# Making a small Gelu from the exponential inside an attention loop, and moving what follows by two steps

## The chip, the cores and the metric

The kernel runs on one core of a Trainium2 chip. The metric is the device time of one execution in microseconds, the median of several runs. Below, PE is TensorE, ACT is ScalarE, DVE is VectorE and POOL is GpSimd.

## The reference, cut to what matters

Two transformer blocks run one after the other on 512 tokens of width 1024, in float32. The second one holds a sparse attention with three branches. The change touches the smallest of them, the compressed branch, in which keys and values of 32 tokens are squeezed into one by a small two-layer network:

```python
def compress_blocks(kr, pos, w1, b1, w2):
    nc = (T - CMP_BLOCK) // CMP_STRIDE + 1            # 31 windows
    idx = np.arange(nc)[:, None] * CMP_STRIDE + np.arange(CMP_BLOCK)[None, :]
    blk = kr[:, idx] + pos[None, None, :, None, :]
    flat = blk.transpose(0, 1, 3, 2, 4).reshape(B, nc, G, CMP_BLOCK * D)
    return jax.nn.gelu(flat @ w1 + b1) @ w2           # hidden width 256; gelu is the tanh form
```

It is called once for keys and once for values. The hidden layer is 256 wide, for two groups of 31 windows each: as the kernel holds it, 128 partitions by 2 (keys, values) x 2 (halves of 256) x 62 = 248 numbers.

## The kernel before, in words

Each large matmul takes its float32 operands as a high and a low part, so that a product is three matmuls: a weight unit of 128x1024 comes by DMA into one of six slots of `stage`, ACT rounds it to `w_hi` (L657), POOL forms `w_lo` as two instructions of 128x512 (L683), and PE uses both.

The second attention (`at2`) is written out by hand as a loop over steps. It has 96 items (a head, a block of 128 queries and a key range). PE, ACT, DVE and POOL each run their own loop over the same step numbers, and wait for each other through semaphores. In step n:

- PE issues the logits of items n and n+1 when n is even (L1074), then the value products of the pair n-6 (`soft_heads`, L1096), the transposes of items n-4 and n-3 (L1121), then a number of matmuls from a list of other work (`FILL2`), and last its hooks. The fill matmuls are the query and key projections of the same layer (`pe_chunk_steps`, L1424): each projection is 24 matmuls into one PSUM bank (bank 6), and the next one waits until DVE has read the bank (`dve_evac2`, L1035).
- DVE runs its early hooks (`dve0`; each `dve_evac2` is one), scales and adds the bias to item n (L1276), normalises item n-1 after ACT's exponential (L1298, L1304), and then runs its late hooks (`dve`).
- ACT takes the exponential of item n-1 (L1211), copies the transposed weights of item n-4 for PE (L1229), and runs its hooks.
- POOL only runs its hooks.

The compressed branch lives in these hooks. `at` is 49, the step in which its first layer's last matmuls are transposed (`pe_hidden`). The Gelu stands at ACT's step 50 (`act_gelu`, L1687), the second layer at PE's step 52 (`pe_second`, L1696 and L1701), its copies at ACT's step 53 (`act_second`), its logits on PE at 54 and 57 (`pe_cmp_s`, L1731), their scaling on DVE at 55 and 58 (`dve_cmp_logits`, L1754), the softmax's steps on DVE from 59 to 66 (`dve_cmp_shift` at 59 and 61, L1764 to L1768; `dve_cmp_probs` at 63 and 65, L1784 to L1792; `dve_cmp_weigh`), its transposes on PE at 66 and 68, the value products on PE at 70, 72, 74 and 76 (`pe_cmp_pv`, L1828), the sums on DVE one step after each (`dve_cmp_add`, L1837), and the split of the result into high and low parts at 78 to 82 (`act_sum_hi`, `dve_sum_lo`). The fill's projections `kb`, `qb0`, `qb1`, `qb2` and `qb3` are read by DVE at the start of steps 52, 56, 64, 72 and 85; the output projection begins as fill in step 86.

Of the kernel before, what the change touches and what calls it, by code (L numbers as in the profile page):

```python
# [35 lines left out]
ALU = mybir.AluOpType  # L36
ACT = mybir.ActivationFunctionType
# [24 lines left out]
NCMP = (T - CMP_BLOCK) // CMP_STRIDE + 1  # L62
# [97 lines left out]


IN_BLOCKS = 68
FILL2 = [0, 8] * 24 + [0, 12] * 4 + [0, 6] * 6 + [3] * 4 + [0] + [2] * 12 + [0]
FILL2 = FILL2 + [4, 3] * 5 + [2, 4, 3, 4, 3, 3]


def fill2_steps(name):

    return sum(12 if n in CMP_AT else 24 for n in FILL2_TASKS[:FILL2_TASKS.index(name) + 1])


def filled(table, count):

    total = 0
    for n, f in enumerate(table):
        total += sum(f) if isinstance(f, tuple) else f
        if total >= count:
            return n
    raise AssertionError(count)
# [6 lines left out]
def turn_steps(g):  # L186

    return 4 * (g + 1) + 3 * max(0, g - 1)
# [22 lines left out]
def build(nc, weights, x_t, params, rows, table_t, bias_line, out_t):  # L211
    with ExitStack() as top:
        def sem(name):
            return top.enter_context(nc.semaphore(name))

        def sb(name, shape, dtype=F32, ctx=top):
            return ctx.enter_context(nc.sbuf_tensor(name, shape, dtype))
# [54 lines left out]
        with ExitStack() as scope:  # L272
# [5 lines left out]
            scratch = sb("scratch", [P, 2 * T], ctx=scope)  # L278
# [21 lines left out]
            hid = sb("hid", [P, 2, 2, 2 * NCMP], ctx=scope)  # L300
# [48 lines left out]
        PS = top.enter_context(nc.psum_tensor("PS", [P, 8, T], F32))  # L349

        def pc(name, k, n=1):
            a, _ = PARAMS[name]
            return par[:, a + k:a + k + n]
# [305 lines left out]
        def act_next(act, u):  # L659

            act_hi(act, u + AHEAD)
# [235 lines left out]
        def queries2(p):  # L897
            return HOME2[f"q{p}" if p < 4 else f"qb{p - 4}"]
# [24 lines left out]
        for p, (kind, c) in enumerate(GROUPS1):  # L923
            q, k = chunk1(2 * p), chunk1(2 * p + 1)
            groups1.append(len(items1))
            for i in reversed(range(TB)) if p == 7 else range(TB):
# [7 lines left out]
                else:  # L934
                    for m in range(2):
                        h = 2 * c + m
# [6 lines left out]
        for p in range(8):  # L943
            c, q = p % 4, queries2(p)
            groups2.append(len(items2))
            for i in range(TB):
                if p < 4:
                    k0, nk, s0 = full(i)
                    for branch in range(2):
                        k = HOME2[("ks", "kw")[branch]]  # L950
                        for g in range(2):
                            h = 4 * g + c
# [6 lines left out]
                else:  # L959
                    k0, nk = max(i - 1, 0) * P, min(i + 1, 2) * P  # L960
                    k = HOME2["kb"]
                    for g in range(2):
                        h = 4 * g + c
# [6 lines left out]
        for items in (items1, items2):  # L970
            pre, at = 0, 0
# [12 lines left out]
        class Attn:  # L984
# [14 lines left out]
        at2 = Attn("at2", items2, groups2, SCALE)  # L999
        qk_evac = [sem("qk_evac1"), sem("qk_evac2")]  # L1000
        ITEM_PS = 3
        cm = {k: sem("cm_" + k) for k in (
            "raw", "kp", "kp_hi", "kp_lo", "mlp", "pre_t", "hid", "kv", "kv_sb", "none", "blank", "z", "zz", "s", "l", "e", "p", "t", "pt", "pv", "used")}
# [10 lines left out]
        def hook(a, engine, step, what):  # L1014
            a.hooks[engine].setdefault(step, []).append(what)
# [9 lines left out]
        for ci in range(4, 16):  # L1025
            at = filled(FILL1, 24 * (ci - 3)) + 1
            hook(at1, "dve0", at, lambda dve, ci=ci: dve_chunk(dve, ci))
            at = NEXT_LATE.get(ci, at + 1)
# [8 lines left out]
        for e, name in enumerate(FILL2_TASKS):  # L1037
            at = filled(FILL2, fill2_steps(name)) + 1
            hook(at2, "act", at + 1, lambda act, u=U_FILL2 + e: act_next(act, u))
# [15 lines left out]
        def pe_attn(pe, a, fill=None, per_item=()):  # L1055
# [6 lines left out]
            def logits(n):  # L1062

                it = items[n]

                pair = [it] if it.kind == "diff" else [it, items[n + 1]]
                maps = [(x, m) for x in pair for m in range(len(x.maps))]
                if it.map0 >= 2:
                    pe.wait_ge(a.s_read, it.map0 - 1)
                for cols in pieces(it.nk):  # L1070
                    last = cols.stop == it.nk
                    for x, m in maps:
                        q, k = x.maps[m]
                        mm = pe.matmul(PS[:, x.bank[m], cols], q, k[:, cols], start=True,  # L1074
                                       stop=(not last or x.kind != "sb"))
                        if last and (x.kind == "soft" or m == 1):
                            mm.then_inc(a.qk_done, 1)
                if it.kind == "sb":
                    for x, m in maps:
                        pe.matmul(PS[:, x.bank[0], x.nk - P:x.nk], ident_r[:, :], mask_r[:, :],  # L1080
                                  start=False, stop=True).then_inc(a.qk_done, 1)
# [42 lines left out]
            if a is at2:  # L1124
                for n in range(len(items) + 6):
# [5 lines left out]
                    if n < len(items) and n % 2 == 0:  # L1131
                        logits(n)
                    if n < IN_BLOCKS:
                        if n >= 6 and n % 2 == 0:
# [455 lines left out]
        for g in range(SPARED):  # L1590
            at = filled(FILL1, 24 * 12 + turn_steps(g)) + 1
            hook(at1, "pool", at, lambda pool, g=g: pool_turn1(pool, g))
        for p in range(8):
            at = groups1[p + 1] if p < 7 else len(items1)
            hook(at1, "pool", at + 4, pool_head_square(p))
            hook(at1, "pool", at + 7, pool_head_scale(p))
        for p in range(7):
            at = groups1[p + 1] + 4
# [6 lines left out]
        for g in range(6):  # L1605
            at = filled(FILL1, 24 * 12 + turn_steps(g)) + 1
# [34 lines left out]
        def pool_windows(s):  # L1641

            def what(pool):
                pool.wait_ge(cm["raw"], 64 * (s + 1))
                if s == 1:
                    wait_unit(pool, fill2_unit("cmp_k3"))
                win = bass.AP(tensor=kpair.tensor, offset=kpair.offset,
                              ap=[kpair.ap[0], [2, 16], [T, 2], [CMP_STRIDE, NCMP]])
                pos = pc("pos_k" if s == 0 else "pos_v", 0, 16).unsqueeze(2).unsqueeze(3).to_broadcast([P, 16, 2, NCMP])
                pool.tensor_tensor(kp.rearrange("p j (g c) -> p j g c", g=2), win, pos, ALU.add).then_inc(cm["kp"], 1)  # L1650
            return what
# [13 lines left out]
        def act_hidden(s):  # L1665
            def what(act):
                act.wait_ge(cm["raw"], 64)
                wait_unit(act, fill2_unit(("cmp_k3", "cmp_v3")[s]))
                act.activation(hidden(s), PS[0:2 * NCMP, 7, 0:CMP_HID], ACT.Copy).then_inc(cm["mlp"], 1)
            return what  # L1670
# [11 lines left out]
        def act_gelu(act):  # L1682
            act.wait_ge(cm["pre_t"], 1)
            for s in range(2):
                for half in range(2):
                    at = s * CMP_HID + half * P
                    act.activation(hid[:, s, half, :], PS[:, 7, at:at + 2 * NCMP], ACT.Gelu_apprx_tanh,  # L1687
                                   bias=pc("b1_k" if s == 0 else "b1_v", half)).then_inc(cm["hid"], 1)
            act.preload_act_table_set("natural_log_exp_and_others")

        def pe_second(pe):

            pe.wait_ge(cm["hid"], 4)
            for g in range(2):
                for half in range(2):
                    pe.matmul(PS[g * HD:(g + 1) * HD, 7, P:P + NCMP], pc("w2_k", half * HD, HD),  # L1696
                              hid[:, 0, half, g * NCMP:(g + 1) * NCMP], start=(half == 0), stop=(half == 1))
            for i in range(4):
                for g in range(2):
                    for half in range(2):  # L1700
                        mm = pe.matmul(PS[32 * i:32 * i + NCMP, 7, g * HD:(g + 1) * HD],  # L1701
                                       hid[:, 1, half, g * NCMP:(g + 1) * NCMP], pc("w2_v", half * HD, HD),
                                       start=(half == 0), stop=(half == 1))
            mm.then_inc(cm["kv"], 1)
# [143 lines left out]
        hook(at2, "dve0", groups2[4], lambda dve: dve.wait_ge(swa_done, 4))  # L1848
        hook(at2, "dve", filled(FILL2, fill2_steps("q3")) + 4, dve_swa_late)
        for s, at in ((0, filled(FILL2, fill2_steps("kc")) + 5), (1, filled(FILL2, fill2_steps("cmp_k3")))):  # L1850
            hook(at2, "pool", at, pool_windows(s))
            hook(at2, "act", at + 3, act_windows(s))
            hook(at2, "pool", at + 4, pool_windows_lo(s))
        for s in range(2):
            hook(at2, "act0", filled(FILL2, fill2_steps(("cmp_k3", "cmp_v3")[s])) + 1, act_hidden(s))
        at = filled(FILL2, fill2_steps("cmp_v3")) + 2
        hook(at2, "pe", at, pe_hidden)
        hook(at2, "act", at + 1, act_gelu)
        hook(at2, "dve0", at + 2, dve_blank_values)
        hook(at2, "pe", at + 3, pe_second)  # L1860
        hook(at2, "act", at + 4, act_second)
        for half in range(2):
# [851 lines left out]
```

## Time and profile before

| | |
|---|---|
| median of 3 runs | 1612.85 us (1612.77 to 1612.92) |
| the profiled execution | 1612.32 us, of which the profile's span is 1610.5 us |
| PE busy | 1589.0 us, 99% of the span |
| PE weight loads | 84% |
| DVE, POOL, ACT busy | 60%, 55%, 47% |
| the second attention's steps 48 to 96 | about 1111 to 1215 us of the span |

PE is busy nearly throughout, so what counts is when PE stands idle and who ends that. The clock granted to PE is full in every slice of the page.

### The profile page before, as it was taken

The page shows a single profiled execution, that of the slowest core. Times are in us where ns is not written, and L with a number is a line of the kernel's source. Part 1 is how long each engine was busy: PE and PEld are TensorE (multiplying, and loading weights), DVE is VectorE, ACT ScalarE, POOL GpSimd, SP SyncE. Part 2 cuts the span into 40 slices and gives each one's busy share as a digit, 9 for nine tenths or more (in the row PEclk, how much of TensorE's full clock was granted, in tenths as well). Part 3 has the DMA queues.
Part 4 walks back from the last instruction along what each step waited for, and adds up shares of the span by engine and source line. Part 5 has one row for each costly group of instructions (what it writes and reads, how often), then busy time and mean ns, then how long its engine had stood idle before and what let it go on. Part 6 is the DMA issues. An engine that isn't in the chain of part 4 may idle for free.

```text
span 1610.5 us, 23966 instructions
## 1 busy us (share of the span) xinstructions
PE 1589.0 (99%) x9196; PEld 1351.1 (84%) x9196; DVE 966.2 (60%) x1592; ACT 761.2 (47%) x1391; POOL 886.7 (55%) x641
## 2 busy tenths in 40 slices
PE   9999999999999999999999999999999999999997
PEld 8787878888888888889998887877767889999886
DVE  7176756884444225878884434576783587886224
ACT  6366655543344324545554323577573445555222
POOL 7424354575445553558889553654114548889650
PEclk9999999999999999999999999999999999999999
DMA  5411103322323222323333222322012323233221
GB/s 209 151 53 53 40 14 105 117 93 93 104 92 104 93 95 76 105 93 105 105 106 105 93 95 74 120 93 80 27 28 92 99 98 105 96 103 106 96 100 53
DMA packets 49682, 147.56 MB, mean 92 GB/s; under 512 B 5152, under 2 KB 13728, under 8 KB 49568
## 3 DMA queue, kind: packets, MB, share of 16 engines
q1 hardware_dynamic: 48232, 143.39, 26.8%
q10 hardware_dynamic: 1336, 2.63, 0.5%
q8 instruction: 74, 1.21, 0.3%
q14 instruction: 40, 0.33, 0.1%
HBM read 142.84 MB, written 3.41 MB: 91 GB/s over the span
## 4 chain that ended last, share of the span: by engine, by line
PE 81%; DVE 2%; POOL 1%; ACT 1%; issue 1%; DMA 1%; SPq 0%; DVEq 0%; ACTq 0%
PE PS L621 14%; PE PS L623 14%; PE PS L622 14%; PE PS L2154 7%; PE PS L2155 6%; PE PS L2156 6%; PE PS L1413 4%; PE PS L582 4%; PE PS L1424 3%; PE PS L590 2%; PE PS L1074 2%; PE PS L1096 2%; PE PS L1121 1%; POOL w_lo L683 1%; DMA stage<-in_weights 1%
## 5 line engine op out<-in xcount | busy, mean ns | idle before, releaser
L683 POOL TENSOR_TENSOR w_lo<-stage,w_hi 128x512 fp32r<-128x512 f32 x402 | 567.3, 1438 | 598.6 <-ACT w_hi L657 597.7
L657 ACT ACTIVATE w_hi<-stage 128x1024 fp32r<-128x1024 f32 x262 | 270.5, 1054 | 303.3 <-DMA stage<-in_weights 289.4
L621 PE MATMUL PS<-H_hi,w_hi 128*128 128x512 f32 x512 | 199.4, 389 | 0.4 <-DVE rcol L1622 0.4
L622 PE MATMUL PS<-H_lo,w_hi 128*128 128x512 f32 x512 | 199.3, 389 | 0.0
L623 PE MATMUL PS<-H_hi,w_lo 128*128 128x512 f32 x512 | 199.2, 389 | 0.0
L621 PE MATMUL PS<-A_hi,w_hi 128*128 128x512 f32 x496 | 193.2, 389 | 0.6 <-DVE A_lo L829 0.6
L623 PE MATMUL PS<-A_hi,w_lo 128*128 128x512 f32 x496 | 193.0, 389 | 0.0
L622 PE MATMUL PS<-A_lo,w_hi 128*128 128x512 f32 x496 | 193.0, 389 | 0.0
L2128 POOL TENSOR_TENSOR S_lo<-S_f,S_hi 128x512 fp32r<-128x512 f32 x90 | 126.5, 1421 | 66.5 <-DVE S_f L1988 37.7
L2128 POOL TENSOR_TENSOR w_lo<-stage,w_hi 128x512 fp32r<-128x512 f32 x90 | 141.8, 1603 | 0.0
L2154 PE MATMUL PS<-F,w_hi 128*128 128x256 f32 x480 | 137.5, 287 | 1.7 <-ACT conv L2047 1.1
L829 DVE TENSOR_TENSOR A_lo<-A_all,A_hi 128x512 fp32r<-128x512 f32 x40 | 52.7, 1321 | 139.6 <-ACT A_hi L765 139.6
L2155 PE MATMUL PS<-F,w_hi 128*128 128x256 f32 x480 | 135.8, 283 | 0.0
L621 PEld LDWEIGHTS PS<-H_hi,w_hi 128*128 128x128 f32 x512 | 96.1, 188 | 20.5 <-DVE rcol L1622 0.7
L623 PEld LDWEIGHTS PS<-H_hi,w_lo 128*128 128x128 f32 x512 | 96.1, 188 | 20.1
L622 PEld LDWEIGHTS PS<-H_lo,w_hi 128*128 128x128 f32 x512 | 96.1, 188 | 20.0
L621 PEld LDWEIGHTS PS<-A_hi,w_hi 128*128 128x128 f32 x496 | 93.1, 188 | 20.8 <-DVE A_lo L829 1.5
L622 PEld LDWEIGHTS PS<-A_lo,w_hi 128*128 128x128 f32 x496 | 93.1, 188 | 19.3
L623 PEld LDWEIGHTS PS<-A_hi,w_lo 128*128 128x128 f32 x496 | 93.1, 188 | 19.2
L2154 PE MATMUL PS<-F,S_hi 128*128 128x256 f32 x360 | 101.9, 283 | 0.0
L2155 PE MATMUL PS<-F,S_hi 128*128 128x256 f32 x360 | 101.9, 283 | 0.0
L2156 PE MATMUL PS<-F,S_lo 128*128 128x256 f32 x360 | 101.9, 283 | 0.0
(295 smaller groups left out, 3583.2 us busy)
## 6 DMA issues: line engine op xcount, KB each, us to landing
stage<-in_weights SPq DMA_DIRECT2D x254, 512.0 KB, 3.4
stage<-in_weights SPq DMA_DIRECT2D x32, 128.0 KB, 2.8
out_t<-Y SPq DMA_DIRECT2D x8, 256.0 KB, 2.0
X<-in_x_t SPq DMA_DIRECT2D x3, 512.0 KB, 8.4
bias_line<-bias_line ACTq DMA_DIRECT2D x1, 1270.0 KB
strip<-bias_line ACTq DMA_DIRECT2D x1, 1024.0 KB, 5.0
stage<-in_weights SPq DMA_DIRECT2D x2, 256.0 KB, 4.1
V<-QF SPq DMA_DIRECT2D x4, 128.0 KB, 2.7
```

Source lines behind the costliest of these rows:

```text
L582: pe.matmul(PS[:, j, :], w[:, (u0 + j) % RING, bass.ts(c, P)], H_hi[:, c, :], start=(k == 0 and w is w_hi), stop=False)
L621: pe.matmul(out, a, h_hi, start=first, stop=False, skip_group_check=skip)
L622: pe.matmul(out, a, h_lo, start=False, stop=False, skip_group_check=skip)
L623: return pe.matmul(out, b, h_hi, start=False, stop=last, skip_group_check=skip)
L657: act.activation(w_hi[:, slot, :], stage[:, slot, :], ACT.Copy).then_inc(hi_done, 1)
L683: lo = pool.tensor_tensor(w_lo[:, slot, cols], stage[:, slot, cols], w_hi[:, slot, cols].bitcast(F32), ALU.subtract)
L829: dve.tensor_tensor(halves_lo(inst, f), product(inst, f), halves_hi(inst, f).bitcast(F32), ALU.subtract).then_inc(a_lo_done, 1)
L1413: mm = pe.matmul(PS[:, j, :], w[:, u % RING, cols], h, start=(g == 0 and x == 0), stop=(g == 7 and x == 2))
L2128: return pool.tensor_tensor(out, raw, hi.bitcast(F32), ALU.subtract)
L2154: pe.matmul(bank, hi[:, cols], where[:, h, k, :], start=(first and k == 0), stop=False, skip_group_check=True)
L2155: pe.matmul(bank, hi[:, cols], where[:, l, k, :], start=False, stop=False, skip_group_check=True)
L2156: mm = pe.matmul(bank, lo[:, cols], where[:, h, k, :], start=False, stop=(k == 3), skip_group_check=True)
```

## The change

The four Gelu instructions become four Identity instructions that only add the bias and bring the hidden layer from PSUM to SBUF. From there x * gelu's factor is worked out as x / (1 + exp(-2 c (x + 0.044715 x^3))): four instructions on POOL form the exponent's argument and bound it, ACT takes the exponential one step later, and three on DVE add one, take the reciprocal and multiply. The request for the exponential's table behind the Gelu goes. All hooks of the branch from `pe_second` on stand two steps later; the projections and the rest of the loop stay where they were.

```diff
+GELU_STEPS = 2
...
-                    act.activation(hid[:, s, half, :], PS[:, 7, at:at + 2 * NCMP], ACT.Gelu_apprx_tanh,
+                    act.activation(hid[:, s, half, :], PS[:, 7, at:at + 2 * NCMP], ACT.Identity,
                                    bias=pc("b1_k" if s == 0 else "b1_v", half)).then_inc(cm["hid"], 1)
-            act.preload_act_table_set("natural_log_exp_and_others")
...
+        def gelu_parts():
+
+            x = hid[:, :, :, :].rearrange("p s h c -> p (s h c)")
+            return x, scratch[:, 0:8 * NCMP]
+
+        def pool_gelu(pool):
+
+            x, t = gelu_parts()
+            pool.wait_ge(cm["hid"], 4)
+            pool.tensor_tensor(t, x, x, ALU.mult).then_inc(cm["hid"], 1)
+            pool.wait_ge(cm["hid"], 5)
+            pool.tensor_scalar(t, t, 2.0 * GELU_C * 0.044715, 2.0 * GELU_C, ALU.mult, ALU.add).then_inc(cm["hid"], 1)
+            pool.wait_ge(cm["hid"], 6)
+            pool.tensor_tensor(t, t, x, ALU.mult).then_inc(cm["hid"], 1)
+            pool.wait_ge(cm["hid"], 7)
+            pool.tensor_scalar(t, t, EXP_BOUND, None, ALU.max).then_inc(cm["hid"], 1)
+
+        def act_gelu_exp(act):
+
+            _, t = gelu_parts()
+            act.wait_ge(cm["hid"], 8)
+            act.activation(t, t, ACT.Exp, scale=-1.0).then_inc(cm["hid"], 1)
+
+        def dve_gelu(dve):
+
+            x, t = gelu_parts()
+            dve.wait_ge(cm["hid"], 9)
+            dve.tensor_scalar(t, t, 1.0, None, ALU.add).then_inc(cm["hid"], 1)
+            dve.wait_ge(cm["hid"], 10)
+            dve.reciprocal(t, t).then_inc(cm["hid"], 1)
+            dve.wait_ge(cm["hid"], 11)
+            dve.tensor_tensor(x, x, t, ALU.mult).then_inc(cm["hid"], 1)
...
-            pe.wait_ge(cm["hid"], 4)
+            pe.wait_ge(cm["hid"], 12)
...
         hook(at2, "act", at + 1, act_gelu)
+        hook(at2, "pool", at + 1, pool_gelu)
+        hook(at2, "act", at + 2, act_gelu_exp)
+        hook(at2, "dve", at + 2, dve_gelu)
         hook(at2, "dve0", at + 2, dve_blank_values)
+        at += GELU_STEPS
         hook(at2, "pe", at + 3, pe_second)
```

On DVE, at the end of step 51 and the start of step 52, these rows stood in a row before (`small`, `stat` are columns of statistics, `B_f` is the home of projection `kb`, `QF` holds the compressed values):

```order
L1710 MEMSET QF 128x512
L1276 ISA L,stat<-PS,strip 128x128
L1276 ISA stat 128x1
L1298 RECIPROCAL stat<-stat 128x1
L1304 TENSOR_SCALAR tmp<-tmp,stat,gates 128x128
L1035 TENSOR_TENSOR B_f<-PS,rstd 128x512
L1276 ISA L,stat<-PS,strip 128x256
```

and these now (lines behind the new functions have other numbers):

```order
L1746 MEMSET QF 128x512
L1277 ISA L,stat<-PS,strip 128x128
L1277 ISA stat 128x1
L1299 RECIPROCAL stat<-stat 128x1
L1305 TENSOR_SCALAR tmp<-tmp,stat,gates 128x128
L1721 TENSOR_SCALAR scratch<-scratch 128x248
L1723 RECIPROCAL scratch<-scratch 128x248
L1725 TENSOR_TENSOR hid<-hid,scratch 128x248
L1036 TENSOR_TENSOR B_f<-PS,rstd 128x512
```

The three new instructions stand ahead of the read of `kb`'s bank.

On ACT, from the end of step 50 to step 52, these stood before:

```order
L1229 ACTIVATE O<-PS 128x512
L1687 ACT_TABLE_LOAD
L1687 ACTIVATE hid<-PS,par 128x62 x4
L1689 ACT_TABLE_LOAD
L1211 ACTIVATE tmp,stat<-L,stat 128x128
L1229 ACTIVATE O<-PS 128x512
L1211 ACTIVATE tmp,stat<-L,stat 128x128
```

and these now:

```order
L1230 ACTIVATE O<-PS 128x512
L1688 ACTIVATE hid<-PS,par 128x62 x4
L1212 ACTIVATE tmp,stat<-L,stat 128x128
L1230 ACTIVATE O<-PS 128x512
L1715 ACTIVATE scratch<-scratch 128x248
L1212 ACTIVATE tmp,stat<-L,stat 128x128
```

Both table loads are gone, and the new exponential stands behind step 51's copy for PE.

On PE, at the end of step 52 and the start of step 53, these stood before:

```order
L1121 MATMUL PS<-ident,sq 128x128 x2
L1696 MATMUL PS<-hid,par 64x31 x4
L1701 MATMUL PS<-par,hid 31x64 x16
L1424 MATMUL PS<-H_hi,w_hi 128x512
L1424 MATMUL PS<-H_lo,w_hi 128x512
```

and these now:

```order
L1122 MATMUL PS<-ident,sq 128x128 x2
L1425 MATMUL PS<-H_hi,w_hi 128x512
L1425 MATMUL PS<-H_lo,w_hi 128x512
L1425 MATMUL PS<-H_hi,w_lo 128x512
```

The second layer has left the place ahead of projection `qb0`'s first matmul; it now follows the transposes of step 54.

## Rows read from the trace of the kernel before

**Rows 1.** Who PE waited for, 1080 to 1290 us: us in total, times, longest

```profile
PE PS L1096 <- ACT O L1229: 1.4, 1, 1.4
PE PS L1424 <- DVE QB L1035: 0.6, 1, 0.6
```

**Rows 2.** Timeline of PE, steps 52 and 53 (start, duration in us)

```profile
1121.82 1.09 PE L1096 MATMUL PS<-O,V 128*64 128x128 f32 x16 [1.38 <-ACT O L1229]
...
1123.22 0.43 PE L1696 MATMUL PS<-hid,par 128*64 128x31 f32 x8
...
1124.90 0.50 PE L1424 MATMUL PS<-H_hi,w_hi 128*128 128x512 f32 x1
```

**Rows 3.** Timeline of ACT, steps 50 and 51

```profile
1117.26 1.28 ACT L1687 ACT_TABLE_LOAD   x1
1118.56 0.92 ACT L1687 ACTIVATE hid<-PS,par 128x62 f32<-128x62 f32 x4
1119.50 1.28 ACT L1689 ACT_TABLE_LOAD   x1
...
1121.19 0.58 ACT L1229 ACTIVATE O<-PS 128x512 f32<-128x512 f32 x1
```

**Rows 4.** Timeline of DVE, steps 50 to 52

```profile
1115.45 1.05 DVE L1304 TENSOR_SCALAR sq<-sq,stat,gates 128x128 f32<-128x128 f32 x1
...
1121.32 0.17 DVE L1298 RECIPROCAL stat<-stat 128x1 f32<-128x1 f32 x1 [4.05 <-ACT tmp L1211]
...
1121.78 0.68 DVE L1035 TENSOR_TENSOR B_f<-PS,rstd 128x512 f32<-128x512 f32 x1
```

**Rows 5.** Timeline of POOL, 1105 to 1140 us

```profile
1113.91 2.51 POOL L683 TENSOR_TENSOR w_lo<-stage,w_hi 128x512 fp32r<-128x512 f32 x2 [0.43 <-ACT w_hi L657]
1125.17 2.54 POOL L683 TENSOR_TENSOR w_lo<-stage,w_hi 128x512 fp32r<-128x512 f32 x2 [8.75 <-ACT w_hi L657]
```

**Rows 6.** Groups by line and shape, whole span (busy us, mean ns)

```profile
L1539 POOL TENSOR_TENSOR scratch<-O 128x512 f32<-128x512 f32 x8 | 8.5, 1064 | 0.5 <-POOL O L1561 0.5
L1359 POOL CAST H_hi<-turn_f 128x512 fp32r<-128x512 f32 x4 | 2.4, 612 | 5.9 <-ACT turn_f L1351 5.7 <-POOL O L1553 0.2
L2307 POOL CAST cdist<-hid 128x128 f32<-128x128 int32 x1 | 0.8, 760 | 0.0
L1196 ACT ACTIVATE L<-L 128x256 f32<-128x256 f32 x8 | 3.3, 418 | 0.3
L1844 DVE TENSOR_SCALAR V<-V 128x256 f32<-128x256 f32 x4 | 0.9, 280 | 0.0
L1632 DVE RECIPROCAL gates<-gates 128x96 f32<-128x96 f32 x1 | 0.8, 752 | 0.0
L1788 DVE RECIPROCAL small<-small 128x16 f32<-128x16 f32 x2 | 0.5, 254 | 0.1
```

**Rows 7.** Timeline of DVE, steps 58 to 64

```profile
1140.73 0.86 DVE L1754 SCALAR_TENSOR_TENSOR L<-cdist,PS 128x124 f32<-128x124 f32 x4
...
1142.57 0.66 DVE L1764 TENSOR_REDUCE small<-L 128x16 f32<-128x496 f32 x1
...
1144.07 0.68 DVE L1276 CUSTOM_DVE_ANT_0 L<-PS,strip 128x512 f32<-128x512 f32 x1
...
1151.09 0.66 DVE L1784 TENSOR_REDUCE small<-L 128x16 f32<-128x496 f32 x1
...
1152.39 0.68 DVE L1035 TENSOR_TENSOR QB<-PS,rstd 128x512 f32<-128x512 f32 x1
```

**Rows 8.** Timeline of PE, steps 60 and 76

```profile
1142.13 1.13 PE L1074 MATMUL PS<-K_f,QF 64*128 64x256 f32 x8
...
1176.17 1.09 PE L1828 MATMUL PS<-scratch,QF 128*64 128x128 f32 x16
```

**Rows 9.** Timeline of DVE, steps 78 and 85

```profile
1179.31 0.48 DVE L1276 CUSTOM_DVE_ANT_0 L<-PS,V,row 128x256 f32<-128x256 f32 x1 [0.62 <-PE PS L1074]
...
1190.25 0.68 DVE L1035 TENSOR_TENSOR QB<-PS,rstd 128x512 f32<-128x512 f32 x1
```

More of the change, by code:

```diff
@@ L1686, in act_gelu @@
                     at = s * CMP_HID + half * P
-                    act.activation(hid[:, s, half, :], PS[:, 7, at:at + 2 * NCMP], ACT.Gelu_apprx_tanh,
+                    act.activation(hid[:, s, half, :], PS[:, 7, at:at + 2 * NCMP], ACT.Identity,
                                    bias=pc("b1_k" if s == 0 else "b1_v", half)).then_inc(cm["hid"], 1)
-            act.preload_act_table_set("natural_log_exp_and_others")
+        EXP_BOUND = -80.0
+        GELU_C = math.sqrt(2.0 / math.pi)
+        def gelu_parts():
[23 more added lines that the diff above has]
+            dve.tensor_tensor(x, x, t, ALU.mult).then_inc(cm["hid"], 1)
         def pe_second(pe):
-            pe.wait_ge(cm["hid"], 4)
+            pe.wait_ge(cm["hid"], 12)
             for g in range(2):
```

## The prediction

> **What bounds the kernel now.** I read the busy shares first: PE is busy 99% of the span, so only what makes PE stand idle, or what adds matmuls, can move the time, and the change adds no matmul. Then I read who PE waits for between 1080 and 1290 us, the second attention and the start of what follows. The longest wait of PE there is one of 1.4 us for ACT's copy, and the next is one of 0.6 us for DVE's read of a projection bank [rows 1]. Then the timelines around both. The first stands right behind the two table loads: ACT loads the Gelu's table at 1117.26, runs four instructions in 0.92 us, loads the old table until 1120.78, takes step 51's exponential, and only then makes the copy, 1121.19 to 1121.77 [rows 3], for which PE waited 1.38 us; PE had been ready at 1121.82 - 1.38 = 1120.44 [rows 2]. So the loads are on the path that sets the end, but PE's own work hides all of them except 1.38 us. After the last output projection the next weights are requested when PE frees their slots, so a shift of PE in this attention moves the rest of the span with it.
>
> **The change part by part.**
> *Removed: two table loads.* ACT's four instructions now start at 1117.26 and end at 1118.18, and the copy of step 51 follows as before 1121.19 - 1120.78 = 0.41 us after them, ready at about 1119.2 (before 1120.44) [rows 2, 3]. The wait of 1.38 us goes; the gain from it is at most that. PE then reaches the end of step 52's transposes at 1123.22 - 1.38 = 1121.84 [rows 2].
>
> *Moved: the second layer.* It took PE from 1123.22 to 1124.90, 1.68 us [rows 2], between these transposes and the first matmul of `qb0`. It now comes in step 54: it costs the same there, but it no longer covers DVE. PE wants the bank of `kb` at 1121.84, not at 1124.90. Before, DVE had read it at 1122.46 (1121.78 + 0.68) [rows 4], 2.4 us early.
>
> *Added: the chain POOL, ACT, DVE.* It starts at 1118.18. POOL is free: its last work ended at 1116.42, and its next came at 1125.17 [rows 5]. POOL's two products are like L1539, a square of 128x512 in 1064 ns: by columns 248/512 x 1064 = 0.52, with a fixed part for each I take 0.56 us. For a tensor-scalar instruction on POOL there is no row; nearest with one input is the cast, 612 ns for 512 columns [rows 6]. By columns alone that is 0.30, with L1539's price it is 0.56; I take 0.40, nearer to the cast. Sum 2 x 0.56 + 2 x 0.40 = 1.92, and 0.06 to 0.08 for each of four hand-overs (POOL starts 0.08 us behind ACT in the timelines): the argument is ready at about 1120.4. The ends are 1.6 us (all by columns) and 2.8 us (all four at the rate of L683 at its slower mean of 1.44 us, 0.70 each). ACT's exponential is L1196's size: 0.42, to 1120.9 [rows 6]. ACT stands still for it from about 1119.2; behind it wait the exponential of item 51 and the copy of item 48, which PE's transposes release only near 1121.9, so nothing is late there.
>
> DVE: the add is 0.28 (L1844). The reciprocal is what counts: 254 ns for 16 columns and 752 ns for 96, so 498/80 = 6.2 ns a column, and for 248 columns 752 + 152 x 6.2 = 1.70 us [rows 6]; its low end is 0.75, the row of 96 columns itself. The product of 248 columns I put at 0.41, from the read of 512 columns of B_f at 0.68 [rows 4], of which half the columns is 0.34 at least. With hand-overs DVE runs from 1120.96 to 1123.4. Behind these three stands the read of `kb` (0.68): done at 1124.03, and PE goes on at 1124.08.
>
> So at equal work: PE begins `qb0` at 1124.08 instead of 1124.90, but still owes the 1.68 us of the second layer: 1124.08 + 1.68 - 1124.90 = **+0.86 us**. PE's wait for ACT of 1.38 us is replaced by one of 2.24 us for DVE (1124.08 - 1121.84). Ends: with the short reciprocal and POOL's low end -0.4, with POOL's high end +1.7.
>
> *A rule weighed.* While POOL's pair of instructions ran until 1116.42, a DVE instruction that began at 1115.45 took 1.05 us and ended in the same moment, 1116.5 [rows 4, 5]; it is 0.3 to 0.4 us long when POOL rests. In the changed kernel the normalisation of item 50 on DVE falls at about 1119, among POOL's four. If DVE has to wait, it is free again long before 1120.96, so I price it at nothing; if instead POOL waits for DVE, the chain grows by one such instruction, 0.35 us. The Trainium skill says in SBUF — State Buffer, section "SBUF: two separate sides", that the shared port pair is an exclusive lock for which whichever instruction started first makes the other stand still; by that rule the sum would be 0.35 us more at worst, and the trace agrees for the side that it shows.
>
> *Two steps later, first stretch.* Up to step 64 DVE is the late one: PE waited 0.6 us for its read of `qb1` [rows 1]. From item 60 (1144.07) to that read (1152.39) DVE needed 8.32 us. Of this `dve_cmp_probs` (1151.09 to 1152.39, 1.30) now comes after it; `dve_cmp_logits` (0.86 less an overlap of 0.08) and one `dve_cmp_shift` (1142.57 to 1144.07, 1.50), which lay before item 60, come into it [rows 7]: 8.32 - 1.30 + 0.78 + 1.50 = 9.30. But DVE can start item 60 at 1143.2, when its logits end [rows 8], and not at 1144.07: 1152.5 against 1152.39, so **+0.1 us**.
>
> *Second stretch.* In steps 78 to 85 DVE works without rest and PE waits for it. One value product of PE (1176.17, 1.02 net of overlap [rows 8]) moves from step 76 to 78, behind the logits of item 78, for which DVE had waited until 1179.31 [rows 9]: DVE starts that stretch 1.0 us sooner. It has one sum more in it (`dve_cmp_add`, 0.6). So its read of `qb3` at 1190.25 [rows 9] comes 0.4 us sooner, and with it the output projection: **-0.4 us**. If DVE is not free by 1178.3, this turns into up to +0.6. The splits at 79 to 82 move to 81 to 84, all still ahead of that read, and cost nothing more.
>
> *Sum:* 0.86 + 0.1 - 0.4 = +0.5 us. The profiled execution (1612.32) would be at 1612.8; the median stands 0.53 above it, so 1612.85 + 0.5 = **1613.3 us**.
>
> **The rivals.**
> *The wait is simply gone* (15%). If DVE's three instructions are short (a reciprocal of 0.75) and POOL's at their low end, PE's wait for `kb` is near 2.24 - 0.95 - 0.3 = 1.0 us, and with the second stretch the kernel gains about 0.8: 1612.0. If DVE would read the bank ahead of the chain, the whole 1.38 would be kept: 1611.1. Against it: the two reciprocal rows lie on one line that leaves little room, and the order on DVE is fixed.
> *The later stretches pay* (20%). DVE is busy nearly without gaps from 1140 on, and small instructions on it grow when POOL forms a low part. If the two-step shift puts more on DVE just before `qb2`'s read and before step 78, PE waits 0.4 there, the -0.4 is lost and the +0.6 comes: 1613.3 + 0.4 + 0.4 + 0.6 = 1614.7.
> *POOL is far slower* (6%), the side of slower by over 0.2%. One row of POOL, a cast of 128 columns, took 760 ns [rows 6], 5.9 ns a column; at that rate the four instructions take 5.9 us, not 1.92, the chain ends 4 us later, and all of it is PE's wait: 1617.3. It decides from where the four take 1.92 + 2.7 = 4.6 us. Against it: that cast converts integers, and every float row is at 1.2 to 2.8 ns a column.
> The Trainium skill, GPSIMD Engine Reference, section 3.1, gives about 2.6 cycles an element for a product of two tensors on this engine, an estimate of 0.54 us for 248 columns, which the rows bear out.
>
> **How the numbers follow.** The forecast (a DVE wait of about 2.2 us in place of ACT's, net 0 to +1.4) has 55%, the rivals 15, 20 and 6, the rest is for what I have not seen. A measurement of this kernel can tell about 0.2%, 3.2 us, from no change. The range reaches from the first rival to just past the second, 1611.7 to 1615.2; the third is left out. Faster by over 0.2% has 2%, slower 6%, within 92%.
>
> **What would show it.** In the changed profile: no table load near 1117; the step-52 value products of PE without a wait; a wait of PE of 1.5 to 3 us for DVE's `B_f` before `qb0`; a reciprocal of 1.6 to 1.8 us; four POOL instructions of 1.6 to 2.8 us together, starting near 1118.2; PE's second layer in step 54. I am wrong if PE has no wait on `B_f`, if the reciprocal is under 1 us, or if new waits of over 1 us in sum stand after step 64.

## The result and the profile after

The changed kernel takes 1616.27 us (median of 13 runs, 1614.86 to 1617.30), the kernel before beside it 1612.78 us (median of 13, 1612.55 to 1613.44): a ratio of 1.0021, 95% interval 1.0013 to 1.0030. It is 3.5 us slower; the forecast said 0.5 us slower, in a range that ended at 1615.2. The profiled execution took 1616.39 us, its span is 1614.6 us.

Who PE waited for in the changed kernel, 1080 to 1290 us (as [rows 1]):

```profile
PE PS L1425 <- DVE B_f L1036: 2.8, 1, 2.8
PE PS L1414 <- DVE QB L1036: 1.0, 1, 1.0
PE PS L1122 <- ACT O L1224: 0.8, 1, 0.8
PE PS L1425 <- DVE QB L1036: 0.6, 1, 0.6
```

The wait of 1.4 us for ACT's copy is gone, and one of 2.8 us for DVE's read of `kb` has come. Two later ones differ. The one of 0.8 us, for ACT's copy in step 72, is new: before, PE waited for nothing there (a wait of 0.3 us for a later copy, at 1188.10, is gone). The one of 1.0 us, for the read of `qb3`, was 0.6 us.

Timeline of PE in the changed kernel, steps 52 and 53 (start, duration), as [rows 2]:

```profile
1120.90 1.09 PE L1097 MATMUL PS<-O,V 128*64 128x128 f32 x16
1121.92 0.44 PE L1122 MATMUL PS<-ident,sq 128*128 128x128 f32 x2
1125.12 0.50 PE L1425 MATMUL PS<-H_hi,w_hi 128*128 128x512 f32 x1 [2.76 <-DVE B_f L1036]
1125.46 0.40 PE L1425 MATMUL PS<-H_lo,w_hi 128*128 128x512 f32 x1
...
1126.40 0.51 PE L1425 MATMUL PS<-H_hi,w_lo 128*128 128x512 f32 x1
1126.71 0.63 PE L1425 MATMUL PS<-H_hi,w_hi 128*128 128x512 f32 x1
1127.14 0.63 PE L1425 MATMUL PS<-H_lo,w_hi 128*128 128x512 f32 x1
```

The step-52 products run without a wait, and `qb0` begins 2.76 us late. Then comes something that no step of the prediction has: from 1126.71 on the same matmul takes 0.63 instead of 0.40 us, and the starts are 0.43 us apart instead of 0.23. Stretches of PE in the changed kernel (from:to, length, busy time and matmuls, granted clock, DMA share, GB/s) say why:

```profile
1122.00:1124.00 2.00, 0.36 (x2) 1.00 0.63 182
1124.00:1126.00 2.00, 0.88 (x4) 1.00 0.22 64
1126.00:1127.00 1.00, 1.00 (x5) 0.76 0.00 0
1127.00:1129.00 2.00, 2.00 (x6) 0.50 0.03 8
1129.00:1130.00 1.00, 1.00 (x8) 0.53 0.00 0
1130.00:1132.00 2.00, 2.00 (x37) 1.00 0.00 0
```

The granted clock is full (2.4 GHz) during the wait and for another 1.4 us, falls to half (1.2 GHz) at about 1126.5, and is full again from 1130: (1 - 0.76) x 2 + 2 + (1 - 0.53) x 2 = 3.4 us at half speed by these rows. From `qb0`'s first matmul to the end of the next step's transposes PE needed 5.91 us (1125.12 to 1131.03), and 4.24 us for the same work before (1124.90 to 1129.14): the clock costs 1.67 us here.

Timeline of POOL, ACT and DVE at the new Gelu, changed kernel:

```profile
1118.65 0.60 POOL L1703 TENSOR_TENSOR scratch<-hid 128x248 f32<-128x248 f32 x1 [1.72 <-ACT hid L1688]
1119.34 0.45 POOL L1705 TENSOR_SCALAR scratch<-scratch 128x248 f32<-128x248 f32 x1
1119.88 0.71 POOL L1707 TENSOR_TENSOR scratch<-scratch,hid 128x248 f32<-128x248 f32 x1
1120.68 0.83 POOL L1709 TENSOR_SCALAR scratch<-scratch 128x248 f32<-128x248 f32 x1
...
1121.54 0.41 ACT L1715 ACTIVATE scratch<-scratch 128x248 f32<-128x248 f32 x1 [2.10 <-POOL scratch L1709]
...
1119.19 0.35 DVE L1305 TENSOR_SCALAR tmp<-tmp,stat,gates 128x128 f32<-128x128 f32 x1
...
1121.99 0.29 DVE L1721 TENSOR_SCALAR scratch<-scratch 128x248 f32<-128x248 f32 x1 [2.44 <-ACT scratch L1715]
1122.31 1.70 DVE L1723 RECIPROCAL scratch<-scratch 128x248 f32<-128x248 f32 x1
1124.05 0.42 DVE L1725 TENSOR_TENSOR hid<-hid,scratch 128x248 f32<-128x248 f32 x1
1124.38 0.68 DVE L1036 TENSOR_TENSOR B_f<-PS,rstd 128x512 f32<-128x512 f32 x1
```

The chain stands as forecast, and the read of `kb` is queued behind it. POOL's part takes 2.86 us from start to end, the largest miss among these rows. The later places in the timeline of PE and DVE, changed kernel, answer to [rows 7] and [rows 9]:

```profile
1156.00 0.68 DVE L1036 TENSOR_TENSOR QB<-PS,rstd 128x512 f32<-128x512 f32 x1
...
1171.21 0.41 PE L1122 MATMUL PS<-ident,sq 128*128 128x128 f32 x2 [0.79 <-ACT O L1224]
...
1182.68 0.48 DVE L1277 CUSTOM_DVE_ANT_0 L<-PS,V,row 128x256 f32<-128x256 f32 x1 [0.62 <-PE PS L1075]
...
1194.23 0.69 DVE L1036 TENSOR_TENSOR QB<-PS,rstd 128x512 f32<-128x512 f32 x1
1194.97 0.50 PE L1414 MATMUL PS<-T_hi,w_hi 128*128 128x512 f32 x1 [1.01 <-DVE QB L1036]
```

**Where the 3.5 us are.** The two profiled executions are already 0.53 us apart ahead of the Gelu (PE's first transposes of the hidden layer start at 1114.26 before and at 1114.79 after), in work that the change does not touch; in the other profiles this lead is 0.36 to 0.91 us. At `qb0` the difference at equal work is 1125.12 + 1.68 - 1124.90 = 1.90, so 1.37 of it is the exchange of waits. The clock adds 1.67: 3.6 us at DVE's read of `qb1` (1156.00 against 1152.39), so steps 58 to 64 add nothing. At the read of `qb3` it is 1194.23 - 1190.25 = 4.0: the second stretch adds 0.4. In sum 1.4 + 1.7 + 0 + 0.4 = 3.5.

### The profile page after: what moved, and what is told of

It reads as the page before. It is cut to its first block, busy times and chain, and to the rows that moved or that the text cites. A ratio compares the mean times of both kernels' runs of the same rounds, so it can differ in the third digit from the quotient of the medians.

```text
span 1614.6 us, 23972 instructions
## 1 busy us (share of the span) xinstructions
PE 1590.9 (99%) x9196; PEld 1352.5 (84%) x9196; DVE 971.6 (60%) x1595; ACT 758.4 (47%) x1390; POOL 889.5 (55%) x645
## 4 chain that ended last, share of the span: by engine, by line
PE 81%; DVE 2%; POOL 1%; issue 1%; ACT 1%; DMA 1%; SPq 0%; DVEq 0%; ACTq 0%
PE PS L622 14%; PE PS L624 14%; PE PS L623 14%; PE PS L2194 7%; PE PS L2195 6%; PE PS L2196 6%; PE PS L1414 4%; PE PS L583 4%; PE PS L1425 3%; PE PS L591 2%; PE PS L1075 2%; PE PS L1097 2%; PE PS L1122 2%; POOL w_lo L684 1%; DMA stage<-in_weights 1%
```

## The experiments

**Theory.** The chain on POOL, ACT and DVE makes PE wait for `kb`; that wait costs its own length, and once more about 1.6 us, because the clock falls behind it. **Rivals:** the loss belongs to the moved second layer and the later stretches (the shift); or what is lost behind the wait is not the clock's.

### Four edits that take the parts of the change apart

*DVE reads the bank ahead of the Gelu.*

```diff
-        hook(at2, "dve", at + 2, dve_gelu)
+        hook(at2, "dve0", at + 3, dve_gelu)
```

> The changed kernel, with DVE's three Gelu instructions one place later: behind the read of projection kb's bank instead of ahead of it. If the loss is PE's wait of 2.8 us for that read and the stretch at half clock behind it, PE has no wait there, the clock stays full, and the time is the changed kernel's 1616.3 less 1.4 (chain) and 1.7 (clock), less the 1.4 of the old wait for ACT that is gone too: about 1611.9. If the two-step shift costs most, it stays over 1615.

Measured: 1612.08 us (1611.78 to 1612.40, 11 runs) beside 1613.08 before, ratio 0.9994 (0.9985 to 1.0003). The stretch from 1118 to 1134 of PE in this kernel (columns as above):

```profile
1118.00:1134.00 16.00, 15.84 (x140) 1.00 0.16 45
```

PE is busy for 15.84 of the 16 us and at full clock. DVE's timeline there:

```profile
1120.60 0.69 DVE L1036 TENSOR_TENSOR B_f<-PS,rstd 128x512 f32<-128x512 f32 x1 [0.82 <-PE PS L1425]
...
1122.55 1.70 DVE L1723 RECIPROCAL scratch<-scratch 128x248 f32<-128x248 f32 x1
```

Against before this kernel is 1.0 us shorter and the changed one 3.5 us longer, so one place in DVE's queue is worth 4.5 us. The interval of the gain reaches past 1, but all 11 executions are shorter than the shortest of the 33 before. The reciprocal is as long as ever; it only no longer stands ahead of what PE wants.

*The reciprocal left out* (the output then lacks the division of the Gelu):

```diff
-            dve.reciprocal(t, t).then_inc(cm["hid"], 1)
-            dve.wait_ge(cm["hid"], 11)
...
-            pe.wait_ge(cm["hid"], 12)
+            pe.wait_ge(cm["hid"], 11)
```

> The changed kernel without the reciprocal (the Gelu's factor is left as its denominator; everything else as it is). DVE's chain is 1.74 us shorter. If PE's wait shortens by that and the clock then stays full: 1616.3 - 1.7 - 1.7 = 1612.9. If the clock falls at half speed after a pause of about 1.0 us too: 1614.6.

Measured: 1613.04 us (1612.64 to 1613.66, 11), ratio 1.0000 (0.9992 to 1.0009); PE's wait is 1.0 us and the clock stays full. Against before that is 0.0 where the changed kernel has 3.5, so leaving out 1.70 us of DVE's work gives back 3.5.

*The shift alone*: the Gelu as before with its two table loads, `GELU_STEPS` at 2. Against the kernel before:

```diff
+GELU_STEPS = 2
...
         hook(at2, "dve0", at + 2, dve_blank_values)
+        at += GELU_STEPS
         hook(at2, "pe", at + 3, pe_second)
```

> The kernel before, Gelu with its two table loads as it was, and only what follows it two steps later. My theory: the shift itself costs 0.4 us (DVE's read of qb3 later): 1613.2. The rival that the shift pays most of the loss gives 1615 or more.

Measured: 1613.35 us (1613.14 to 1613.74, 11), ratio 1.0002 (0.9993 to 1.0010): 0.27 us over before, not to be told from none by the interval, and of the sign and size that the trace gives the second stretch. The later waits of 0.8 and 1.0 us stand in this kernel too, so they come with the shift. The first rival, that the shift makes the loss, falls.

*The new Gelu without the shift:*

```diff
-GELU_STEPS = 2
+GELU_STEPS = 0
```

> The changed kernel with what follows left at its old steps. PE then waits for the chain ahead of the second layer, at 1123.2 less 1.4, for about 2.3 us, and the read of kb is covered by the second layer as before. If a wait of that length brings the clock down wherever it stands: 1612.8 + 1.0 + 1.7 = 1615.5. If the clock stays full: 1613.8.

Measured: 1614.02 us (1613.42 to 1615.34, 11), ratio 1.0008 (0.9999 to 1.0017). The values fall into two groups, six at 1613.4 to 1614.0 and five at 1614.6 to 1615.3. The profiled one (1614.02) has the full clock throughout and a wait of 2.16 us of the second layer for DVE. The two groups lie near the two numbers expected, 1613.8 and 1615.5; this was the first sign that the clock is a matter of the single execution. No profile shows the fall in this kernel: that it stands behind the upper group is inferred from the times.

### How the loss goes with the length of the wait

*Half a reciprocal* (124 of 248 columns; the output lacks the rest):

```diff
-            dve.reciprocal(t, t).then_inc(cm["hid"], 1)
+            dve.reciprocal(t[:, 0:4 * NCMP], t[:, 0:4 * NCMP]).then_inc(cm["hid"], 1)
```

> The changed kernel with the reciprocal taken of the first 124 of the 248 columns only (the rest keeps its denominator). PE's wait for DVE's read of kb should be 2.76 - 0.77 = 2.0 us. If the clock then mostly stays full, as with the 2.2 us of the run without the shift: 1616.3 - 0.8 - 1.7 = 1613.8. If it falls each time: 1615.5.

Measured: 1615.46 us (1614.06 to 1615.95, 11), ratio 1.0015 (1.0007 to 1.0024), beside 1612.86 before. Two executions at 1614.1, nine at 1615.1 to 1616.0; the profiled one is of the two, with a wait of 2.0 us and a full clock. Here too the fall in the others is inferred from the times, 1.4 us between the groups.

*A second reciprocal behind the first:*

```diff
+            dve.reciprocal(scratch[:, 8 * NCMP:16 * NCMP], t).then_inc(cm["hid"], 1)
...
-            pe.wait_ge(cm["hid"], 12)
+            pe.wait_ge(cm["hid"], 13)
```

> The changed kernel with a second reciprocal of 248 columns into an unused place, ahead of the read of kb. PE's wait grows by 1.74 to 4.5 us. If the clock's price is one stretch of about 3.4 us at half speed however long the wait: 1616.3 + 1.7 = 1618.0. If the price grows with the wait, 1619 or more.

Measured: 1618.38 us (1618.09 to 1619.06, 5), ratio 1.0036 (1.0024 to 1.0048). PE's timeline in the profiled execution (1619.02):

```profile
1126.50 0.79 PE L1425 MATMUL PS<-H_hi,w_hi 128*128 128x512 f32 x1 [4.31 <-DVE B_f L1036]
```

Its stretches of PE, the granted clock behind the number of matmuls:

```profile
1124.00:1126.00 2.00, 0.00 (x0) 0.97 0.12 36
1126.00:1127.00 1.00, 0.50 (x1) 0.50 0.00 0
...
1130.00:1132.00 2.00, 2.00 (x7) 0.50 0.03 8
1132.00:1134.00 2.00, 2.00 (x22) 0.83 0.00 0
```

Here the clock falls while PE still stands, at about 1125.9, and stays at half for 6.8 us, twice as long as in the changed kernel. The part of it that lies in the wait costs nothing. From `qb0`'s first matmul to the end of the next step's transposes PE needs 7.15 us (1126.50 to 1133.65) instead of 4.24: 2.9 us of clock. This is one of two executions at 1619.0 to 1619.1; the other three lie at 1618.1 to 1618.4, and no profile shows one of those. By the medians the kernel is 2.0 us over the changed one (5.5 against 3.5 over before): 4.31 - 2.76 = 1.55 us of longer wait and some 0.5 us more of clock. So both numbers expected are missed by some: behind a wait this long the clock can cost more than one stretch of 3.4 us.

### The clock by itself

These two and the changed kernel once more ran side by side on one chip, before 1613.02 us (1612.71 to 1613.72, 25 runs).

*The wait filled.* PE transposes the identity 18 times in its wait, to a place that nobody reads:

```diff
+        def pe_filler(pe):
...
+            pe.wait_ge(cm["hid"], 4)
+            for _ in range(FILLERS):
+                pe.transpose(PS[:, 7, 0:P], ident[:, :], ident[:, :])
...
+        hook(at2, "pe", at + 3, pe_filler)
         at += GELU_STEPS
```

> The changed kernel, with 18 transposes of the identity matrix on PE just ahead of its wait for the bank of kb, into a region of PSUM that nobody reads before the second layer overwrites it: about 0.13 us each (the step's eight transposes take 1.09 us), 2.3 us in all, so they end at about 1124.6, before DVE's read of the bank does (1125.1). DVE, ACT and POOL do what they did and PE goes on at the same moment; only what PE does meanwhile differs. Theory (1.6 us of the loss is the half-speed stretch that follows PE's idle wait): no stretch below full clock near 1126, wait on B_f under 1 us, median about 1.5 us under the changed kernel's beside it, 1614.8. Rival (those 1.6 us belong to something else around the projection of qb0, or the stretch has to do with the matmuls that follow, not with the idle time): median as the changed kernel's, 1616.2, or more.

> The changed kernel itself, unaltered, for its spread on the same chip as the two runs beside it: median 1616.2, most executions at 1615.9 to 1616.6, about one in ten at 1614.9 (those in which the clock stays at full speed), and the profiled one shows a wait on B_f of 2.7 to 2.8 us.

Measured: with the filler 1614.85 us (1614.45 to 1614.97, 11), ratio 1.0011 (1.0002 to 1.0020); the changed kernel again 1616.26 us (1614.78 to 1617.71, 11), ratio 1.0020 (1.0011 to 1.0029), one execution at 1614.78 and ten at 1615.8 or above. PE's timeline with the filler, and a stretch of PE behind the wait:

```profile
1122.36 2.13 PE L1732 MATMUL PS<-ident 128*128 128x128 f32 x18
1125.28 0.50 PE L1426 MATMUL PS<-H_hi,w_hi 128*128 128x512 f32 x1 [0.80 <-DVE B_f L1037]
...
1127.01 0.39 PE L1426 MATMUL PS<-H_lo,w_hi 128*128 128x512 f32 x1
...
1126.00:1128.00 2.00, 2.00 (x11) 1.00 0.00 0
```

`qb0` begins no sooner (1125.28 against 1125.12), and yet the kernel is 1.41 us shorter, in all 11 executions alike. Eighteen useless instructions on the engine that bounds the kernel buy 1.4 us: what is lost behind the wait is the clock's, and it falls for want of work on PE. The two executions of the changed kernel that are nearest to it, 1614.78 and 1614.86 in the two series, took the filler's time without a filler, and their mean clock, 0.999, is the highest of their series. What remains over before, 1614.85 - 1613.02 = 1.83, is 1.37 of exchanged waits and 0.4 of the second stretch, with 0.06 left.

The profile of the changed kernel's second series (1616.26) has the same wait, but the clock falls at another moment:

```profile
1125.17 0.80 PE L1425 MATMUL PS<-H_hi,w_hi 128*128 128x512 f32 x1 [2.76 <-DVE B_f L1036]
...
1124.00:1126.00 2.00, 0.83 (x2) 0.72 0.25 64
```

By the second row it falls at about 1124.9, while PE still stands, 1.6 us sooner than in the first profile; it again stays at half for 3.4 us.

*The kernel before, delayed.* Nothing of the change, only three reciprocals on DVE ahead of the read of `kb`, whose result nobody uses:

```diff
...
+            for k in range(3):
+                dve.reciprocal(scratch[:, 0:8 * NCMP], hid[:, :, :, :].rearrange("p s h c -> p (s h c)")).then_inc(cm["hid"], 1)
+                dve.wait_ge(cm["hid"], 5 + k)
...
+        hook(at2, "dve", at + 2, dve_delay)
```

> The kernel before, untouched but for three reciprocals of 248 columns on DVE (5.1 us, their result unused) in step 52, behind item 51's work and ahead of the read of the bank of kb. That read then ends at about 1127.7, PE wants it at 1124.9: a wait of about 2.9 us. No step is moved, both table loads stand, PE's wait of 1.4 us for ACT too. Theory (any idle wait of PE of this length here costs its own length and in most executions about 1.6 us of clock behind it): median 1612.85 + 2.9 + 1.6 = 1617.3, with a half-speed stretch of 3.4 us shortly behind the wait. Rival (the loss behind the wait comes with the Gelu's new form or the two-step shift): 1615.7 and full clock in nearly all executions.

Measured: 1617.22 us (1615.76 to 1617.87, 9), ratio 1.0024 (1.0014 to 1.0034): three at 1615.8, six at 1617.0 to 1617.9. PE's timeline in the profiled one:

```profile
1128.09 0.69 PE L1424 MATMUL PS<-H_hi,w_hi 128*128 128x512 f32 x1 [2.77 <-DVE B_f L1035]
1128.57 0.63 PE L1424 MATMUL PS<-H_lo,w_hi 128*128 128x512 f32 x1
```

In this execution already the first matmul is slow. The stretches of PE in it:

```profile
1126.00:1128.00 2.00, 0.00 (x0) 1.00 0.00 0
1128.00:1130.00 2.00, 1.92 (x5) 0.56 0.00 0
1130.00:1132.00 2.00, 2.00 (x7) 0.59 0.00 0
1132.00:1134.00 2.00, 2.00 (x20) 1.00 0.00 0
```

By the second row the clock falls at about 1128.2, just behind the start of the first matmul. The old Gelu with the same idle wait has the same loss, 2.8 us of wait and 1.4 of clock (1617.22 - 1613.02 = 4.2). So neither the Gelu's form nor the shift is needed for it.

The Trainium skill, TensorE: Matmul & The Clock Gate, section "What's actually happening", says that TensorE's clock is gated down by default and that recent activity of the engine is what releases it; by that rule a wait should be dearer than its length, and the traces agree: here 4.2 us for a wait of 2.8.

### POOL's last instruction

POOL's maximum took 0.83 us and its multiply-and-add 0.45, on the same columns. Is it the form with a single operation that is slow?

```diff
-            pool.tensor_scalar(t, t, EXP_BOUND, None, ALU.max).then_inc(cm["hid"], 1)
+            pool.tensor_scalar(t, t, EXP_BOUND, 0.0, ALU.max, ALU.add).then_inc(cm["hid"], 1)
```

> The changed kernel with POOL's last instruction written with two operations (maximum, then adding zero). In the changed kernel it took 0.83 us with one operation, and the other tensor-scalar 0.45 with two. If the one-operation form is the slow one, it takes 0.45, the chain and PE's wait are 0.4 us shorter, and the time is 1615.9 or, where the clock stays full more often, less. If it is the place or the operation, 0.83 and 1616.3 stay.

Measured: 1616.62 us (1615.35 to 1617.68, 9), ratio 1.0024 (1.0015 to 1.0033), beside 1612.86 before. POOL's timeline:

```profile
1120.82 1.05 POOL L1709 TENSOR_SCALAR scratch<-scratch 128x248 f32<-128x248 f32 x1
```

A second operation makes it longer, not shorter, so that idea falls; the multiply-and-add still takes 0.45 us. What is left is the operation, the maximum, or the instruction's place behind the product; no run has the maximum in another place. The profiled execution (1615.35) waits 3.0 us and keeps the full clock; the other eight lie at 1616.4 or above.

### The version that keeps what the change could bring

With the read ahead of the Gelu (as in the first experiment), the two-step shift kept only for the second layer up to the logits (their second half is one step late), and everything from `dve_cmp_shift` on back at its old steps:

```diff
-        hook(at2, "dve", at + 2, dve_gelu)
+        hook(at2, "dve0", at + 3, dve_gelu)
...
-            hook(at2, "pe", at + 5 + 3 * half, pe_cmp_s(half))
-            hook(at2, "dve", at + 6 + 3 * half, dve_cmp_logits(half))
+            hook(at2, "pe", at + 5 + 2 * half, pe_cmp_s(half))
+            hook(at2, "dve", at + 6 + 2 * half, dve_cmp_logits(half))
+        at -= GELU_STEPS
```

> The run with the read first, and of the hooks behind the second layer only the first ones two steps late: the second half of the branch's logits stands one step later than before the change (PE 58, DVE 59), and everything from the first shift on at its old step. If the two-step shift of DVE's softmax and sums is what costs 0.3 to 0.4 us (PE's waits of 0.8 for ACT's copy and 1.0 for qb3), these waits return to 0.3 and 0.6 and the time is 1612.1 - 0.4 = 1611.7. If the shift was free, 1612.1; if PE now waits for DVE in step 58, more.

Measured: 1611.84 us, ratio 0.9993 (0.9985 to 1.0002), beside 1612.86 before (11 of its 12 executions lie at 1611.65 to 1612.23, one at 3161.61, for which the record has no cause, is left out of the ratio). Who PE waited for, 1080 to 1290 us:

```profile
PE PS L1425 <- DVE QB L1036: 0.6, 1, 0.6
PE PS L1414 <- DVE QB L1036: 0.6, 1, 0.6
...
PE PS L1122 <- ACT O L1224: 0.3, 1, 0.3
```

The new waits are gone, the old one for the table loads too. Against before it is 1.0 us shorter where the changed kernel is 3.5 longer; but the interval reaches past 1, so this gain is likely and not proved, though the 11 executions are all shorter than the shortest of the 27 before.

## Why the prediction was right and wrong

**The step that failed** is the one that prices the new wait: "PE's wait for ACT of 1.38 us is replaced by one of 2.24 us for DVE", net 0.86 us, entered into the sum as a length and nothing else: the clock behind the wait was put at nothing, without a reason. The wait was found where it was forecast, for the reason forecast. But with a wait of that length most executions have a stretch of 3.4 us at half clock, and that costs 1.4 us (the filled wait against the changed kernel) to 1.67 us (the profiled pair). No term, no bound and no rival held this; the range ended 1.1 us under the median. The waits of before could not have shown the price: the only long one near there is 1.38 us, and the clock is full behind it. But the end of that trace, behind PE's last matmul, shows what standing still does to the clock (a row of PE's timeline and two stretches of PE, kernel before):

```profile
1600.57 1.03 PE L519 MATMUL PS<-sq,ones 128*128 128x256 f32 x4
...
1606.00:1608.00 2.00, 0.00 (x0) 0.72 1.02 395
1608.00:1610.00 2.00, 0.00 (x0) 0.50 0.84 323
```

PE is done at 1601.6, and at about 1606.9 the clock falls to half. In the thirteen profiles this last fall comes 2.1 to 5.3 us after PE stopped; in the four that have a fall in the loop it comes 2.5 to 4.2 us after PE stopped, whether PE has resumed or not. A cost of that sort should have widened the range upwards.

**Mis-sized terms.** POOL's four instructions were put at 1.92 us and took 0.60 + 0.45 + 0.71 + 0.83 = 2.59. The first two are 0.04 and 0.05 us over their price (0.56, 0.40), the second product is 0.15 over its 0.56; the fourth, taken as like the second, took twice its 0.40. Both products also took longer than the estimate of 0.54 us that stands beside the third rival. The sum of 2.59 is inside the stated ends of 1.6 and 2.8; with the hand-overs the four ran for 2.86 us. This gives the wait 2.76 instead of 2.24 us: 1.37 net, inside the stated ends of -0.4 and 1.7. The second stretch was forecast at -0.4 and came at +0.4: DVE was to start item 78 1.0 us sooner at equal work and started it 0.24 sooner (1182.68 against 1179.31, less the 3.61 that had come before). PE, whose logits it waits for, had lost 0.79 us in the new wait for ACT's `O` at 1171.21. These transposes of step 72 had no wait before:

```profile
1167.87 0.44 PE L1121 MATMUL PS<-ident,sq 128*128 128x128 f32 x2
```

With the value product of step 70 moved away PE came there 1.0 us sooner, and ACT's copy was not ready; 1.02 - 0.79 = 0.23 is what reached item 78. No step of the prediction had this. From item 78 to the read of `qb3` DVE needed 11.55 us instead of 10.94, the 0.6 of the added sum as forecast: -0.24 + 0.61 = +0.37. The rival "the later stretches pay" had named the loss of the -0.4 and a +0.6, of which 0.4 came; its wait at `qb2` was not seen. The sign "new waits of over 1 us in sum after step 64" came too: 0.79, and 0.42 more at `qb3` (less the 0.3 and 0.35 us of two waits of before that are gone). The medians resolve this term hardly: the shift alone gives 0.27, and the kernel that puts the late steps back has the shorter waits, yet stands as far under its before as the one that doesn't (1.0 us both).

Two slips changed nothing. The second longest wait between 1080 and 1290 us was not one of 0.6 but one of 0.8 us for POOL's `w_lo`, 0.9 in the changed kernel. And the terms of the first rival add up to a gain of 0.7 us, 1612.2, not 0.8 and 1612.0.

**Right.** The table loads and the wait of 1.38 us went, worth its full length only if nothing takes its place: with the read first and the late steps back the gain is 1.0 us. The reciprocal took 1.70 us, as the line through 16 and 96 columns said; the add 0.29, the product 0.42, the exponential 0.41. The lost cover of the second layer was right, and the first stretch was 0.0 instead of 0.1. The case "DVE reads the bank ahead of the chain" was put at 1611.1 with the whole of 1.38 kept; the two kernels of that kind came at 1612.08 and 1611.84. The lock between POOL and DVE cost nothing that can be seen: DVE's normalisation at 1119.19 took 0.35 us as elsewhere, though POOL's product ran until 1119.25 and POOL's next instruction began at 1119.34. Whether that one stood still within its 0.45 us is not shown.

**Open.** Whether the clock falls differs between executions of one kernel, and nothing in the profile says beforehand which: by the two groups of times, with waits of 2.0 us it fell in nine of eleven, of 2.2 in five of eleven (four, if the one at 1614.56, whose mean clock is that of a full one, is none), of 2.8 in 21 of 24 executions of the changed kernel and six of nine of the delayed one, of 3.0 in eight of nine, of 4.3 in all five; with waits of up to 1.4 us in none. The waits are those of the profiled executions, and only for 2.8 and 4.3 us does a profile show the fall. The length of the wait is therefore not all that decides. Some executions lie about 1 us higher still: 1617.1 to 1617.7 in three of the 24 of the changed kernel, 1617.5 to 1617.7 in three of the nine with 3.0 us. Their mean clock over the run is 0.996 or 0.997, as in the profiled one of the doubled reciprocal with its 6.8 us at half (0.996), so they probably had a longer stretch too; no profile shows one.

## What to carry to other kernels

In a kernel like this, with PE busy 99% of the time, a wait of two or more microseconds is to be priced at its length and about 1.5 us more, and the range should hold the cases with and without it. By these times two waits of 1.4 us should be cheaper than one of 2.8, but no run tried that. Before a chain is put on an engine that also empties banks, look at what is queued behind it and for whom: here one place in DVE's queue was worth 4.5 us, more than every term of the change. If a wait can't be removed, work of no use on PE in it is worth trying: here 18 transposes gave back 1.4 us.

## What the runs showed of the hardware

- The clock need not fall in the wait. It fell 1.4 us after PE had resumed in the first profile of the changed kernel, 0.3 us before PE resumed in its second, and 0.15 us after in the delayed kernel of before. Each stretch at half clock lasted some 3.4 us; with the wait of 4.3 us it was 6.8 us.
- On POOL a tensor-scalar instruction over 248 float columns takes 0.45 us for multiply and add, 0.83 for a maximum, 1.05 for a maximum and an add (the last two in another place of the chain); the product of a tile with itself took 0.60 us, of two tiles 0.71.
- DVE's reciprocal is linear from 16 to 248 columns, 6.2 ns a column: 254 ns for 16, 752 for 96, 930 for 124 and 1700 for 248. Three in a row took 5.17 us.
